# Mixer steps of a two-layer decoder dealt out over other tiles of the weight stream, with one expression rewritten

## What is computed

```python
h = rmsnorm(x, g_mix)
a_v, a_g, b_b, b_c, b_x, c_g, c_x, d_q, d_k, d_v, d_g = split(h @ w_in, 11)
y_a, new_conv_a = causal_dwconv(a_v * sigmoid(a_g), conv_a, w_conv_a)      # width 31
y_a = silu(layernorm(y_a, ln_a_g, ln_a_b))
y_b = b_b * causal_dwconv(b_c * b_x, conv_b, w_conv_b)                     # width 3
xr = causal_dwconv(c_x, conv_c, w_conv_c) + b_conv_c                       # width 4
r, ig = sigmoid(xr @ w_gate_a + b_gate_a), sigmoid(xr @ w_gate_x + b_gate_x)
log_a = -8 * r * softplus(-lam);  a = exp(log_a)
b = sqrt(max(-expm1(2 * log_a), 0)) * (ig * xr)                            # sqrt(1 - a^2)
y_c = scan(h = a * h + b) * gelu(c_g)
o, new_s = retention(rope(d_q), rope(d_k) / sqrt(128), d_v, ret_s)         # 4 heads, chunks of 128
y_d = silu(d_g) * o * rsqrt(mean(o * o) + eps)
x = x + concat(y_a, y_b, y_c, y_d) @ w_out
x = x + (silu(causal_dwconv(rmsnorm(x) @ w_ffn_gate)) * (rmsnorm(x) @ w_ffn_up)) @ w_ffn_down
```

## Time and profile before

| | us |
|---|---|
| median of 3 runs | 2444.77 (2442.79 to 2444.85) |
| the profiled execution | 2442.28 |
| its span, first to last instruction | 2440.5 |
| PE busy | 2343.5 (96%) |
| DVE busy | 1713.6 (70%) |
| ACT busy | 1004.5 (41%) |

### The profile page before, as it was taken

The page is one execution under the profiler, slowest core; times in us unless marked ns, Lnnn a source line. Parts: engine busy times, 40 slices in busy tenths (PEclk is TensorE's granted clock), DMA queues, the critical chain, the costliest instruction groups (busy, mean ns, idle before and its releaser), DMA issues.

```text
span 2440.5 us, 48608 instructions
## 1 busy us (share of the span) xinstructions
PE 2343.5 (96%) x18842; PEld 2321.7 (95%) x18842; DVE 1713.6 (70%) x2620; ACT 1004.5 (41%) x1095; POOL 0.2 (0%) x4
## 2 busy tenths in 40 slices
PE   7998989999999999999999988999999999999996
PEld 7997989999999999999998978999999999999995
DVE  6894686766666666666669947767666766666666
ACT  5332544434434444434443326344443443444433
POOL 0000000000000000000000000000000000000000
PEclk9998999999999999999999989999999999999998
DMA  7553455555555555555464534555555555555552
GB/s 249 169 162 128 156 160 180 182 182 181 181 179 182 182 180 180 183 179 181 161 196 158 168 125 144 175 185 181 182 180 180 180 181 181 180 180 180 180 181 97
DMA packets 118824, 424.22 MB, mean 174 GB/s; under 512 B 15457, under 2 KB 15713, under 8 KB 118753
## 3 DMA queue, kind: packets, MB, share of 16 engines
q1 hardware_dynamic: 111312, 405.80, 50.9%
q10 hardware_dynamic: 7440, 17.44, 2.0%
HBM read 413.71 MB, written 9.48 MB: 173 GB/s over the span
## 4 chain that ended last, share of the span: by engine, by line
PE 87%; DVE 8%; DVEq 2%; ACT 1%; issue 1%; DMA 0%; ACTq 0%
PE bank L475 28%; PE bank L476 28%; PE bank L477 28%; DVE wl L708 3%; DVE av L689 2%; PE bank L584 1%; PE bank L577 1%; ACT wh L192 1%; DVEq L690 1%; DVEq L861 1%; DVE q L907 1%; DVE xl L702 0%; PE bank L595 0%; PE bank L612 0%; DVEq L966 0%
## 5 line engine op out<-in xcount | busy, mean ns | idle before, releaser
L475 PE MATMUL bank<-xh,wh 128*128 128x264 f32 x4224 | 1217.0, 288 | 50.3 <-DVE wl L708 30.6
L708 DVE TENSOR_TENSOR wl<-raw,wh 128x1024 fp32r<-128x1024 f32 x768 | 938.6, 1223 | 439.7 <-ACT wh L422 224.0
L476 PE MATMUL bank<-xl,wh 128*128 128x264 f32 x4224 | 1208.9, 286 | 0.0
L477 PE MATMUL bank<-xh,wl 128*128 128x264 f32 x4224 | 1207.8, 286 | 0.0
L475 PEld LDWEIGHTS bank<-xh,wh 128*128 128x128 f32 x4224 | 808.6, 191 | 59.5 <-DVE wl L708 32.3
L422 ACT ACTIVATE wh<-raw 128x1024 fp32r<-128x1024 f32 x480 | 509.5, 1062 | 828.5 <-PE bank L477 828.5
L476 PEld LDWEIGHTS bank<-xl,wh 128*128 128x128 f32 x4224 | 809.2, 192 | 0.4
L477 PEld LDWEIGHTS bank<-xh,wl 128*128 128x128 f32 x4224 | 804.4, 190 | 0.0
L192 ACT ACTIVATE wh<-raw 128x1024 fp32r<-128x1024 f32 x288 | 302.7, 1059 | 466.3 <-PE bank L477 455.7
L475 PE MATMUL bank<-hh,wh 128*128 128x264 f32 x1408 | 399.4, 284 | 7.2 <-DVE hl L1034 6.6
L477 PE MATMUL bank<-hh,wl 128*128 128x264 f32 x1408 | 401.1, 285 | 0.0
(11 more groups left out here) (189 smaller groups left out, 1057.9 us busy)
## 6 DMA issues: line engine op xcount, KB each, us to landing
raw<-in_weights SPq DMA_DIRECT2D x768, 512.0 KB, 3.4
x<-in_x_in SPq DMA_DIRECT2D x4, 528.0 KB, 6.6
out_y<-x ACTq DMA_DIRECT2D x4, 528.0 KB, 2.6
s_own<-in_ret_state ACTq DMA_DIRECT2D x4, 512.0 KB, 4.7
k<-in_ret_state ACTq DMA_DIRECT2D x4, 512.0 KB, 4.9
out_new_ret_sample<-s_own ACTq DMA_DIRECT2D x4, 512.0 KB, 4.0
out_new_ret_sample<-k ACTq DMA_DIRECT2D x4, 512.0 KB, 2.8
dg<-in_ffn_state ACTq DMA_DIRECT2D x2, 528.0 KB, 6.1
```

Source lines behind the costliest of these rows:

```text
L475: pe.matmul(out, w_hi, rh, start=first, stop=False)
L476: pe.matmul(out, w_hi, rl, start=False, stop=False)
L477: return pe.matmul(out, w_lo, rh, start=False, stop=last)
L708: tt(wl[:, i, :], raw[:, i, :], wh[:, i, :].bitcast(F32), ALU.subtract).then_inc(lo_made, 1)
```

## The change

The three tables are written anew, and some steps are cut in pieces so that they can be dealt out. PE's instructions are the same in kind and number; nine of its steps stand behind other tiles.

- The taps of `conv_a` go out seven per tile, none on the two tiles with `rope`, over tiles 9 to 26 (before: eight per tile over tiles 8 to 23).
- The outer products' operand gets a tile of its own, `vd`, where it shared `u`, which `conv_a` reads. On DVE `s_new(h)` stands behind tile 25 + h (before: 26 + h). On PE `outer(h)` stands behind tile 25 + h and `read_state(h)` behind 26 + h; the first two of each stood there before, the later ones one or two tiles further on. The two `column_sums` move from behind tiles 25 and 28 to 27 and 29.
- `conv_c` runs in pieces over tiles 27 to 29, its bias in the first tap's instruction.
- `head_sums` and `gates` move from behind tiles 32, 34, 35 to 30, 31, 32, with ACT's roots, SiLUs, sigmoids and `h_decay` moved ahead likewise; the reciprocal of `head_norm` is taken head by head in a tile `inv`.
- 1 - a^2 is tanh times (1 + a^2), with a^2 from ACT (a `Square` in `h_decay`), where it was 2t/(1 + t) with a reciprocal on DVE.
- `recur` is behind tile 36, `conv_b` behind tile 39; before both were behind tile 39. `w_out` reads the parts of the mix in the order in which they are now made.
- The scratch space for DMAs that software describes is made smaller, to make room; the kernel has none of these.

```diff
         kv8 = sb("kv8", [B, 2, HEADS, P])
+        vd = sb("vd", [B, B, CH])
+        inv = sb("inv", [P, 4, T])
...
-                    i = act.activation(e[:, :, :], bank[:, 4:8, 0:T], ACT.Sqrt, scale=1.0 / CH, bias=eps_t)
+                    i = act.activation(inv[:, :, :], bank[:, 4:8, 0:T], ACT.Sqrt, scale=1.0 / CH, bias=eps_t)
                     i.then_inc(S["o_std"].sem, 1)
...
                     i.then_inc(S["t_tanh"].sem, 1)
+                    on("a_exp", l)
+                    on("t_tanh", l)
+                    act.activation(q[:, :, :], ag[:, :, :], ACT.Square).then_inc(S["a_sq"].sem, 1)
 
...
                          (15, swap(k, 15, "k_swap", "q_rope")), (20, h_vt), (21, h_kv8), (23, h_rp), (24, h_o),
-                         (26, lambda: store_s(0)), (26, h_ln_sq), (27, lambda: store_s(1)), (27, reload_s(2)),
-                         (28, h_gelu), (28, reload_s(3)), (29, h_ln_std), (29, lambda: store_s(2)), (30, h_ya),
-                         (31, lambda: store_s(3)), (31, h_o8), (32, h_dg), (32.5, h_ostd),
-                         (34, gate(q, "ga", "ba", "r_sig")), (35, h_s_out), (35, gate(k, "gx", "bx", "i_sig")),
-                         (36, h_decay), (37, h_mix(1, 4, 4, v[:, :, :], "yd", 1)), (38, h_load_fs), (39, h_bsqrt),
-                         (40, h_mix(2, 8, 4, e[:, :, :], "yc", 1)), (44, h_store_par)]
+                         (25.5, lambda: store_s(0)), (26.5, lambda: store_s(1)), (26.5, reload_s(2)),
+                         (27.5, lambda: store_s(2)), (27.5, reload_s(3)), (28, h_ln_sq), (28, h_gelu),
+                         (28.5, lambda: store_s(3)), (29.5, h_ln_std), (29.5, h_o8), (30.5, h_ostd),
+                         (31, h_ya), (31, h_dg), (31.5, gate(q, "ga", "ba", "r_sig")), (32, h_s_out),
+                         (32.5, gate(k, "gx", "bx", "i_sig")), (33.5, h_decay), (35, h_bsqrt),
+                         (35.5, h_mix(1, 4, 4, v[:, :, :], "yd", 1)), (37, h_load_fs),
+                         (37.5, h_mix(2, 8, 4, e[:, :, :], "yc", 1)), (44, h_store_par)]
                 plan += [(40 + m, h_mix(3 + m, 12 + m, 1, u[:, m, :], "yb", m + 1)) for m in range(4)]
                 plan += [(44 + kk, lambda kk=kk: h_x(kk)) for kk in range(KT)]
...
-                                      vd_v[:, 4 * c:4 * c + 4, :].rearrange("p b v -> p (b v)"), start=True, stop=True)
+                                      vd[:, 4 * c:4 * c + 4, :].rearrange("p b v -> p (b v)"), start=True, stop=True)
                     i.then_inc(S["outer"].sem, 1)
...
 
-                hooks = {20: [turn_kv], 21: [scores], 22: [chunk_states], 24: [outputs],
-                         25: [lambda: outer(0), column_sums(av, "conv_a", "ln_mean")],
-                         26: [lambda: read_state(0), lambda: outer(1)], 27: [lambda: read_state(1)],
-                         28: [column_sums(e, "ln_sq", "ln_var"), lambda: outer(2)],
-                         29: [lambda: read_state(2), lambda: outer(3)],
-                         31: [lambda: read_state(3)], 32: [head_sums],
-                         34: [gates(0, "o_std", "ga")], 35: [gates(1, "r_sig", "gx")]}
+                hooks = {20: [turn_kv], 21: [scores], 22: [chunk_states], 24: [outputs], 25: [lambda: outer(0)],
+                         26: [lambda: read_state(0), lambda: outer(1)],
+                         27: [lambda: read_state(1), lambda: outer(2), column_sums(av, "conv_a", "ln_mean")],
+                         28: [lambda: read_state(2), lambda: outer(3)],
+                         29: [lambda: read_state(3), column_sums(e, "ln_sq", "ln_var")], 30: [head_sums],
+                         31: [gates(0, "o_std", "ga")], 32: [gates(1, "r_sig", "gx")]}
 
                 def norm_ready(base):
...
-                        on("mix_lo", l, {0: 1, 4: 3, 8: 2}[kk])
+                        on("mix_lo", l, {0: 1, 4: 2, 8: 3}[kk])
                     if kk >= 12:
...
-                def conv_a(n):
+                def conv_a(first, last):
+
                     def f():
-                        i = taps(av, u, lambda m, j: pw("wa", m, j), WA, range(2 * n, min(2 * n + 2, WA)))
-                        if n == 15:
-                            i.then_inc(S["conv_a"].sem, 1)
+                        for i in range(first, last):
+                            n, m = divmod(i, 4)
+                            w = pw("wa", m, WA - 1 - n)
+                            if m == 0:
+                                dve.drain()
+                            if n == 0:
+                                dve.tensor_scalar(av[:, m, 0:SEQ], u[:, m, 0:SEQ], w, None, ALU.mult)
+                            else:
+                                stt(av[:, m, n:SEQ], u[:, m, 0:SEQ - n], w, av[:, m, n:SEQ], ALU.mult, ALU.add)
+                        if last == 4 * WA:
+                            dve.drain().then_inc(S["conv_a"].sem, 1)
                     return f
 
...
-                    taps(ag, cx, lambda m, j: pw("wc", m, j), WC, range(WC))
-                    for m in range(4):
-                        dve.tensor_scalar(ag[:, m, :], ag[:, m, :], pw("bc", m), None, ALU.add)
-                    dve.drain().then_inc(S["xr"].sem, 1)
+                    dve.drain()
+                    tt(ag[:, :, SEQ:T], ag[:, :, SEQ:T], rows("bc").broadcast_to([P, 4, B]), ALU.add)
+
+                def conv_c(n):
+
+                    def f():
+                        for m in range(4):
+                            w = pw("wc", m, WC - 1 - n)
+                            if n == 0:
+                                dve.tensor_scalar(ag[:, m, 0:SEQ], cx[:, m, 0:SEQ], w, pw("bc", m), ALU.mult, ALU.add)
+                            else:
+                                stt(ag[:, m, n:SEQ], cx[:, m, 0:SEQ - n], w, ag[:, m, n:SEQ], ALU.mult, ALU.add)
+                        i = dve.drain()
+                        if n == WC - 1:
+                            i.then_inc(S["xr"].sem, 1)
+                    return f
 
                 def ln_center():
...
 
-                def head_norm():
-                    on("o_std", l)
+                def head_inverse(*heads):
+                    def f():
+                        on("o_std", l)
+                        for h in heads:
+                            dve.reciprocal(inv[:, h, :], inv[:, h, :])
+                    return f
+
+                def head_gate():
                     on("dg_silu", l)
                     tt(v[:, :, :], v[:, :, :], dg[:, :, :], ALU.mult)
-                    dve.reciprocal(e[:, :, :], e[:, :, :])
-                    dve.drain()
-                    tt(v[:, :, :], v[:, :, :], e[:, :, :], ALU.mult).then_inc(S["yd"].sem, 1)
+
+                def head_norm():
+                    dve.drain()
+                    tt(v[:, :, :], v[:, :, :], inv[:, :, :], ALU.mult).then_inc(S["yd"].sem, 1)
 
                 def gated_in():
...
 
-                    on("t_tanh", l)
-                    dve.tensor_scalar(q[:, :, :], e[:, :, :], 1.0, None, ALU.add)
-                    dve.drain()
-                    dve.reciprocal(q[:, :, :], q[:, :, :])
-                    dve.drain()
-                    stt(q[:, :, :], e[:, :, :], 2.0, q[:, :, :], ALU.mult, ALU.mult)
+                    on("a_sq", l)
+                    stt(q[:, :, :], q[:, :, :], 1.0, e[:, :, :], ALU.add, ALU.mult)
                     dve.drain()
                     dve.tensor_scalar(q[:, :, :], q[:, :, :], 0.0, None, ALU.max).then_inc(S["b_sq"].sem, 1)
...
-                         8: [glu(3), conv_a_samples], 12: [rope(q, "q_swap", "q_rope", 1.0)],
-                         16: [rope(k, "k_swap", "k_rope", CH ** -0.5)], 20: [keys], 21: [masked],
-                         22: [prompt_states], 24: [lambda: v_diag(0), conv_c], 26: [s_new(0), ln_center],
-                         27: [s_new(1)], 28: [s_new(2)], 29: [s_new(3)], 30: [ln_scale],
-                         31: [lambda: mix_lo(0, 0, 4, av[:, :, :])], 34: [head_norm], 36: [gated_in],
-                         37: [b_square, lambda: mix_lo(1, 4, 4, v[:, :, :])], 39: [conv_b, recur]}
-                for n in range(16):
-                    after.setdefault(8 + n, []).append(conv_a(n))
+                         8: [glu(3), conv_a_samples], 9: [conv_a(0, 7)], 10: [conv_a(7, 14)], 11: [conv_a(14, 21)],
+                         12: [rope(q, "q_swap", "q_rope", 1.0)], 13: [conv_a(21, 28)], 14: [conv_a(28, 35)],
+                         15: [conv_a(35, 42)], 16: [rope(k, "k_swap", "k_rope", CH ** -0.5)],
+                         17: [conv_a(42, 49)], 18: [conv_a(49, 56)], 19: [conv_a(56, 63)],
+                         20: [conv_a(63, 67), keys, conv_a(67, 75)], 21: [conv_a(75, 80), masked, conv_a(80, 85)],
+                         22: [conv_a(85, 88), prompt_states, conv_a(88, 92)], 23: [conv_a(92, 99)],
+                         24: [lambda: v_diag(0), conv_a(99, 109)], 25: [conv_a(109, 111), s_new(0), conv_a(111, 115)],
```

(19 more changed lines are left out.)

## The result

The changed kernel takes **2382.78 us**, the median of four runs (2379.15 to 2383.21), against 2444.81 of the kernel before: a ratio of 0.9742 [0.9727, 0.9758], 62.0 us less. The forecast was 2381, with 2362 to 2402 about it. The profiled execution of the changed kernel is its fastest, 2379.15 against 2442.28 before, 63.1 us less.

The account below looks back on a forecast made before the run. PE bounds the kernel; its waits and slow clock cost 88.6 us. From 2442.3, 87.6 removed and 24.2 added (12.1 per layer) give 2378.9; the median's 2.5 makes some 2381 us, range 2362 to 2402 at 0.8.

Parts of the forecast that it names:

- PE's own steps: Tiles 14 to 42: PE's mixer instructions cost 32.4 us per layer beyond the weight matmuls, and stay.
- Taps and ropes: Tiles 14 to 19: seven taps per tile, none beside a rope, end late low parts; 4.7 + 4.3 us removed per layer.
- State updates: Tiles 26 to 28: updates a tile earlier end PE's waits before reads; 20.4 us removed per layer, slack 1.8.
- rival 4: Slower than before: ACT's queue stands at the reload of head 2 or 3 until a late store lands; chance 0.02.
- The pairs: Behind tiles 26, 27, 28: a read beside an outer product lowers PE's clock without waits; 3 x 1.66 = 5.0 us per layer.
- rival 1: The clock holds behind read and outer product and behind 3 us holes; only waits are paid: 2368 us, chance 0.15.
- rival 2: The clock stays down from tile 26 to 30, 21 us in place of 5: 2413 us, chance 0.08.
- Head sums: Behind tile 30: PE waits 1.5 us per layer for ACT's root of the variance and square of o.
- The second gates: Behind tile 32: PE waits 3.1 us for ACT's 10.6 us chain, plus 1.6 of slow clock, per layer.
- A table load at its own 1.28: ACT's chains before head sums and gates: each load costs its 1.28 us alone, without the skill's extra drain.
- Rival 3: Changing ACT's set costs more than its load, lengthening waits by 3.8 us per layer: 2389 us, chance 0.04.
- The end: Tiles 39 to 41: dropping the reciprocal and parting `recur` from `conv_b` removes 12.4 us per layer; 0.9 charged for a late low part.

Follow-up runs that it names:

- best: Changed kernel with outer products of heads 1 to 3 mid-tile, ACT's root and square one `hi` earlier, and second gates one tile later: 2361.43 us.
- e4_apart: Changed kernel with outer products of heads 1 to 3 in the middle of tiles 27 to 29, their DVE updates behind the tile's other work: 2370.47 us.
- after_again: The changed kernel itself, unaltered, run again on another chip as base for three later kernels: 2383.32 us.
- e5_root: Changed kernel with ACT's root of the variance and square of o one chunk earlier in ACT's order: 2379.85 us.
- e2_updates: Changed kernel with the four state updates one tile later on DVE, stores and reloads half a tile later, PE's reads unmoved: 2451.94 us.

## Why the prediction was right, step by step

- **PE's own steps, 32.4 per layer, as the floor.** Right: `best` comes within 2.8 of it, at clock 1.00 throughout.
- **Taps and ropes, 9.0 per layer removed.** Right: nothing is lost at tiles 14 to 19, and undoing the edit costs 17.5, for 2 x 9.0 forecast.
- **State updates, 20.4 per layer removed.** Right in what the change removes: no read waits. The slack was forecast at 1.8 and is 2.1. The store lands after 2.8 us, earlier than the 4.0 before, so ACT's queue never stands at a reload, and rival 4 found nothing to build on. What the prediction didn't see is that the move of the reads makes the stretch dearer than before, 38.2 per layer, without that of the updates.
- **The pairs, three losses of 1.66, 5.0 per layer.** Right in mechanism and place: the clock falls behind each of the three, and `e4_apart` takes it away, for 12.3 us in both layers. By 40.11 as the price without loss the pairs cost 4.5 and 6.0 in the profiled execution and 6.0 twice in `after_again`. So the size is up to 1.0 short per layer. Both of the rivals about them are out: the clock doesn't hold (rival 1), and it doesn't stay down from tile 26 to 30 (rival 2), since 204.90 to 213.00 ran at 1.00.
- **Head sums, 1.5.** Measured 1.3 by the row.
- **The second gates, 3.1 and 1.6 for the clock.** The wait is 3.0, and the chain that had been added up to 10.6 takes 10.7: ACT runs without a gap from 240.57 to 250.99, 10.4, and starts 0.25 behind the end of tile 31. The 1.6 is the term that was mis-sized for the profiled execution: the clock stayed up there. In `after_again` it fell in one layer, in `e5_root` in both, and in `e2_updates` for longer than the 1.6 allows. So the prediction's step from a hole of 3 us to a slow clock isn't a rule, and rival 1's second half is true in some executions.
- **A table load at its own 1.28.** Right: the load at 248.11 ends at 249.39, the sigmoids start at 249.40, and the load itself starts 0.02 behind the `hi`. The drain of some 1.38 us that the Trainium skill adds to each change of set (ScalarE: Activation LUTs, "What ACT_TABLE_LOAD costs") is not in these rows. Rival 3 would have needed a cost beside the load, and the waits it would have lengthened came out at 1.3 and 3.0, no longer than forecast.
- **The end, 12.4 removed and 0.9 charged.** Right: the window over the end is 0.9 over its seven tiles, with 0.6 idle, and the reciprocal with its addition costs 15.1 of twice 12.4 when it is put back.
- **DVE's busy time, down by some 17.** It is 1699.1, 14.5 less than the 1713.6 before, so 2.5 less than forecast; nothing in the sum rests on it.

The 12.1 charged per layer were 11.2 and 12.7 with the tenths. The forecast's closeness owes something to luck, two errors of opposite sign: the pairs charged too low and the gates' clock too high; each is below the 7 us by which runs of this kernel differ.

**What stays open:** why the clock stays down longer behind the first pair of one layer than of another, why a hole of 3.0 us lowers the clock in one execution and not in the next, and whether a read and an outer product in the other order would lower it too. The undone parts don't add up to the gain (17.5 + 69.2 + 15.1 = 101.8 against 62.0), since undoing the updates costs more than the kernel before ever lost; what the updates alone would bring, with the reads where they were, was not run.

## What to carry to other kernels

Where one engine does most of the time at a constant pace, price its own work from stretches without waits, subtract it, and list what is left by tile: that list is what a new schedule can gain, and it also shows what the gain will uncover. Follow the chain on the next engine instruction by instruction up to the point where the first one asks for it; counted so, the new waits came out within 0.3 us. And count light matmuls, those of one column or of few rows, as a risk of their own: half a tile of dense ones between a read and an outer product was enough here.

## What the runs showed of the hardware

- **PE's clock fell without any wait.** Sixteen matmuls of one moving column (1.84 us) and four of eight rows (1.98 us) next to each other brought it from 2.4 to 1.2 GHz for a while; four tiles with three such pairs took 44.6 to 46.2 us in two profiles, and 40.1 with the pairs taken apart, the same instructions in both. The prediction had read this from one tile of the kernel before; that parting them would save it whole was new. The Trainium skill (TensorE: Matmul & The Clock Gate, "Why this matters for your kernels") advises to avoid PE idling between bursts of matmuls; here PE was never idle, so that advice alone would not have found it.
- **The same program keeps the clock in one execution and loses it in the next**, behind the same hole of 3.0 us: 1.00 over the 10 us from the second gates of the first layer in the changed kernel's profile, 0.83 in that of `after_again`.
- **"issue" in the list of waits can hide an engine.** The second gates wait for several things; the wait stood under "issue", 6.1 us, while ACT's last instruction ended 0.1 us before PE went on.
